# Down-projection weight loads of a mixture-of-experts loop issued by ScalarE instead of SyncE

## The reference, cut to what matters

```python
def expert_block(args):
    tok, e = args
    xb = t_pad[tok]
    hdn = jax.nn.silu(xb @ w_gate[e]) * (xb @ w_up[e])
    return hdn @ w_down[e]
```

## Time and profile before

| | us |
|---|---|
| median of 3 runs | 2498.84 (2497.75 to 2510.98) |
| the profiled execution's own time | 2495.0 |
| its span, first to last instruction | 2493.5 |
| TensorE matmul busy | 2087.8 (84%) |
| TensorE weight loads busy (beside the matmuls) | 1250.4 (50%) |
| VectorE busy | 1192.6 (48%) |
| ScalarE busy | 491.0 (20%) |
| GpSimd busy | 106.6 (4%) |
| DMA, mean over the span | 265 GB/s |

### The profile page before, as it was taken

One profiled execution on the slowest core, in us unless ns is written; L12 is line 12 of the kernel. 1 busy time (PEld: TensorE's weight loads), 2 busy tenths in 40 slices (PEclk: granted clock), 3 DMA queues, 4 the chain that ended last, 5 costly groups with the idle time before them and its releaser, 6 DMA issues. The chain is left out here.

```text
span 2493.5 us, 27613 instructions
## 1 busy us (share of the span) xinstructions
PE 2087.8 (84%) x9926; PEld 1250.4 (50%) x9926; DVE 1192.6 (48%) x1851; ACT 491.0 (20%) x513; POOL 106.6 (4%) x147
## 2 busy tenths in 40 slices
PE   0893898999999999989579966988888888888888
PEld 0211686777777777777368854333333333333332
DVE  0205667777777777777445454322222233222223
ACT  1103233333233333333234421000000000000000
POOL 0000000000000000000064000000000000000000
PEclk9997899999999999999789967999999999999999
DMA  3593565647465656566355543999999999999997
GB/s 121 168 305 101 171 183 159 207 139 223 136 209 153 197 157 193 157 194 186 139 175 198 186 169 140 421 422 422 422 422 422 422 422 422 422 422 422 422 422 322
DMA packets 300553, 660.45 MB, mean 265 GB/s; under 512 B 19984, under 2 KB 190480, under 8 KB 246112
## 3 DMA queue, kind: packets, MB, share of 16 engines
q1 hardware_dynamic: 293696, 635.51, 68.9%
q0 software_dynamic: 6672, 24.29, 2.8%
q10 hardware_dynamic: 144, 0.10, 0.0%
HBM read 653.33 MB, written 6.52 MB: 265 GB/s over the span
## 5 line engine op out<-in xcount | busy, mean ns | idle before, releaser
L1495 PE MATMUL bank<-wt,xe 128*64 128x512 f32 x2048 | 464.6, 595 | 111.9 <-DMA wt<-in_moe_w_up 108.5
L1301 PE MATMUL bank<-hTh,whi 128*128 128x512 f32 (+1 forms) x1296 | 455.6, 352 | 82.0 <-DVE wlo L832 59.8
L1302 PE MATMUL bank<-hTl,whi 128*128 128x512 f32 (+1 forms) x1296 | 446.3, 344 | 0.0
L1303 PE MATMUL bank<-hTh,wlo 128*128 128x512 f32 (+1 forms) x1296 | 445.9, 344 | 0.0
L1228 DVE TENSOR_TENSOR x<-x,bank 128x512 f32<-128x512 f32 x256 | 158.4, 681 | 544.6 <-PE bank L1482 544.6
L1495 PEld LDWEIGHTS bank<-wt,xe 128*64 128x64 f32 x2048 | 157.8, 136 | 412.8 <-issue 409.1
L1301 PEld LDWEIGHTS bank<-hTh,whi 128*128 128x128 f32 x1296 | 253.6, 196 | 130.3 <-issue 77.8
L1302 PEld LDWEIGHTS bank<-hTl,whi 128*128 128x128 f32 x1296 | 254.1, 196 | 26.5
L1303 PEld LDWEIGHTS bank<-hTh,wlo 128*128 128x128 f32 x1296 | 253.0, 195 | 27.8
L1520 PE MATMUL bank<-wt,hdn 128*64 128x512 f32 x1024 | 226.8, 595 | 1.4 <-DVE hdn L1240 1.4
L832 DVE TENSOR_TENSOR wlo<-raw,whi 128x2048 fp32r<-128x2048 f32 x81 | 185.2, 2287 | 82.3 <-ACT whi L636 80.4
(11 more groups left out here) (273 smaller groups left out, 1873.1 us busy)
## 6 DMA issues: line engine op xcount, KB each, us to landing
wt<-in_moe_w_gate SPq DMA_DIRECT2D x128, 1024.0 KB, 23.4
wt<-in_moe_w_up SPq DMA_DIRECT2D x128, 1024.0 KB, 25.5
wt<-in_moe_w_down SPq DMA_DIRECT2D x128, 1024.0 KB, 22.4
raw<-in_ada_w SPq DMA_DIRECT2D x96, 1024.0 KB, 5.0
raw<-in_ssm_w_in SPq DMA_DIRECT2D x81, 1024.0 KB, 5.8
raw<-in_ssm_w_out SPq DMA_DIRECT2D x32, 1024.0 KB, 4.8
bc<-cum_d POOLq DMA_DIRECT2D x32, 512.0 KB, 5.0
y_d<-ybuf POOLq DMA_DIRECT2D x32, 128.0 KB, 4.6
```

What stands on the lines that cost most here:

```text
L1301: pe.matmul(bank[:, 0:width], wh[:, k, :], hTh[:, k, 0:width], start=(k == 0), stop=False)
L1302: pe.matmul(bank[:, 0:width], wh[:, k, :], hTl[:, k, 0:width], start=False, stop=False)
L1303: last = pe.matmul(bank[:, 0:width], wl[:, k, :], hTh[:, k, 0:width], start=False, stop=(k == KC - 1))
L1495: last = pe.matmul(banks[0][SLOTS * h:SLOTS * h + SLOTS, :], xe[:, k, :], wt[2 * q + h][:, FF * i:FF * i + FF], start=(k == 0), stop=(k == ...
```

## The change

The function `down` and the waits of its loads move from SyncE's program to ScalarE's. SyncE keeps the gate and up loads. The waits (`s_xg` for block 0, `s_dn` for the rest), the buffers and the semaphores that the loads raise are the same. ScalarE now reads the block's expert number itself in every turn of the loop. Nothing changes on TensorE, VectorE and GpSimd.

```diff
@@ SyncE
-            def down(e, f):
-                sp.dma_start(wt[2 * NQ + f][:, :], w_down[e, :, f:f + 1, :].rearrange("o p f n -> (o p) (f n)")
-                             ).then_inc(s_wt[2 * NQ + f], 16)
...
             sp.wait_ge(s_xg, KC)
-            for f in range(FC):
-                down(slice(0, 1), f)
             for h in range(2):
...
                 for j in range(2 * NQ):
                     sp.wait_ge(s_gu[j % 2], b * NQ + (j // 2 + 1 - NQ))
                     up_gate(bass.ds(e, 1), j)
-                for f in range(FC):
-                    for h in range(2):
-                        sp.wait_ge(s_dn[h], b * FC + (f + 1 - FC))
-                    down(bass.ds(e, 1), f)
@@ ScalarE
+            def down(e, f):
+                act.dma_start(wt[2 * NQ + f][:, :], w_down[e, :, f:f + 1, :].rearrange("o p f n -> (o p) (f n)")
+                              ).then_inc(s_wt[2 * NQ + f], 16)
+
+            act.wait_ge(s_xg, KC)
+            for f in range(FC):
+                down(slice(0, 1), f)
             act.wait_ge(s_tab, 1)
...
             expert(0)
             with act.Fori(1, nblk) as b:
+                e = act.value_load(itab[0:1, bass.ds(b, 1)], min_val=0, max_val=NE - 1)
+                for f in range(FC):
+                    for h in range(2):
+                        act.wait_ge(s_dn[h], b * FC + (f + 1 - FC))
+                    down(bass.ds(e, 1), f)
                 expert(b)
```

## The result

| | us |
|---|---|
| kernel before, median of 20 runs | 2497.65 (2491.2 to 2510.98) |
| changed kernel, median of 20 runs | 2511.53 (2497.83 to 2522.74) |
| ratio | 1.0053, 95% interval 1.0038 to 1.0068 |
| the profiled execution's own time, before and after | 2495.0 and 2520.34 |
| span, before and after | 2493.5 and 2518.6 |

A forecast was written before the change was run, and what follows sets the result against it. The expert loop was taken as bound by its loads at 422 GB/s, with TensorE having 4.2 us to spare per block. Terms 0 + 0 + 0 + 8.8 + 0 on 2498.84 gave 2507.6 us, range 2497.0 to 2516.0.

The forecast's parts named there:

- The two issue terms: SyncE issuing four loads fewer and ScalarE four more per block: each worth 0 on the path.
- Down loads in another ring: End of the kernel: down loads pass waiting pairs, so the last pair lands 8.8 us later, at 2474.8 instead of 2466.0.
- the ends of 6.7 and 9.9: Bounds on the last pair's later landing: 6.7 us without any wait in that block, 9.9 as the latest possible.
- The fixed point of the working: End of the loads: total bytes are unchanged and engines never idle, so the last byte still passes at about 2473.7.
- The 27 to 74: Split of bytes between GpSimd's and SyncE's queues in an earlier row, set against the even split used for the sum.
- TensorE's clock: Last pair: a gathered 4.2 us wait might lower the clock, costing 0 to 3 us; taken as 0.
- the latest landing together with the slow clock: End of the kernel: 9.9 + 3 us, another way to the slower side; loss of rate or slow clock had 0.21.
- the slower rival: Slower by over 0.5%: rate lost with two rings, 2513.5 us, or latest landing with slow clock; chance 0.21.
- Nothing moves: Rival: loads served in issue order or pairs first; last up load lands at 2466.0, time 2498.8; chance 0.14.
- The engines lose rate with two rings: Rival in the loop: 418 GB/s against 422 costs 5.9 us, with the tail 14.7, so 2513.5; chance 0.21 including slow clock.
- A gain in rate: Rival in the loop: two rings raise the rate 3.5% to 437 GB/s, for a time of 2486; chance 0.05.
- The sum: Whole kernel: 0 + 0 + 0 + 8.8 + 0, giving 2507.6 us, counted as the same.

The follow-up runs named there:

- the short fill: Changed kernel plus 6 filling matmuls on TensorE ahead of the last block's last pair of loads: median 2508.29 us, ratio 1.0032, loop time 965.2 us.

## Why the prediction was right, and where it was not

*The two issue terms, 0 and 0: right.* SyncE's up issue fell from a median of 602 ns to 381, as its queue pushes back less, and that was worth nothing. ScalarE took its four issues without delay to anyone:

```profile
2465.84 5.49 ACTq L754 DMA_DIRECT2D wt<-in_moe_w_down  x4
2495.07 0.60 ACT L766 ACTIVATE gsb<-bank 128x512 f32<-128x512 f32 x1 [33.17 <-PE bank L1496]
```

From the end of the last issue at 2471.3 to the copy there are 23.7 us of room, and the copy waits for TensorE, not the reverse.

*Down loads in another ring, 8.8 us: right in mechanism, measured 9.2*, inside the ends of 6.7 and 9.9. The fixed point of the working held best: the last byte passes 936.1 us behind the loop's start, expected 935.9. That the two figures lie within 0.4 us is in part luck, as two details inside the working were off and cancelled. The first down issue of the last block came at 2465.84, 915.0 us into the loop, 2.1 earlier than the 917.1 that 2473.7 - 18.8 gives. The last pair's load landed 22.35 us after it instead of 19.9, as the block's waits were 0.80 + 6.28 and not 4.2. That load took 28.64 us from its issue, more than the 26 that the prediction gave as the most. Four down loads of a block, issued over 5.15 us, land as follows:

```profile
DMA to landing us min/median/max: 9.1/14.0/17.8
```

So the fourth landed 23 us behind the first issue. An even split with nothing left over from before gives 19.9 and the 2.2 us of landing, 22.1. The Trainium skill, page "DMA: Bandwidth & Descriptors", section "Queues, rings and completion order", has each DMA engine take turns between its rings by packet. By that rule the split is even, and this trace agrees to about 1 us, and by the bytes of each ring while both had work:

```profile
q10 hardware_dynamic: 344, 2.56, 51.1%
q1 hardware_dynamic: 341, 2.51, 50.2%
```

These are packets, MB and share from 2471 to 2483 us. The 27 to 74 of the earlier trace rows, between GpSimd's queue and SyncE's, did not hold for these two. The order of single packets is not visible here. The section "Issuing engines are not separate DMA queues" of that page of the Trainium skill has it that several issuing engines save only issue time. The unchanged 422 GB/s bears out that nothing is gained, but the sentence leaves out what decided here: loads in different rings land in another order.

*TensorE's clock, taken as 0 of 0 to 3: wrong, and the one step that failed.* The text said "I take 0, as 4.2 is nearer to 3.42". Both halves fail. The wait was not 4.2 us in each block: it gathers in every second one, and the last block has 0.80 + 6.28 us. In a group of four blocks near the end the waits of some 0.8, 6.3 and 3.7 us, with two slow pairs at 3 us extra each, make up the 16.8 us that TensorE has to spare. And 3.42 us was no bound: behind a wait of 3.70 us the clock fell here, and behind shorter ones too (last section). Nor did the row with 5.24 us of the earlier trace rows show a fall: the clock had stood at 0.50 well before it.

```profile
1460.00:1500.00 40.00, 22.77 (x96) 18.79 (x96) 20.54 (x61) 10.75 (x20) 0.00 (x0) 0.50 0.28 108
1500.00:1516.00 16.00, 3.79 (x16) 2.81 (x16) 13.26 (x41) 0.00 (x0) 0.00 (x0) 0.50 0.00 1
```

The size "up to 3 us" was right: 6.61 - 3.65 = 2.96, and the short fill took 2.6 of it back. I had named "the latest landing together with the slow clock" as a side branch of the slower rival. That is nearly what happened (9.2 + 3.0), and it belonged in the forecast.

*Nothing moves: refuted*, by down loads that land after 13.1 us and not 22.4, and by the last block's row.

*The engines lose rate with two rings: refuted.* From 1700 to 2400 us of the changed kernel:

```profile
DMA packets 40543, 295.30 MB, mean 422 GB/s; under 512 B 4498, under 2 KB 4498, under 8 KB 4498
...
q1 hardware_dynamic: 26901, 195.86, 67.2%
q10 hardware_dynamic: 13642, 99.44, 34.1%
```

The kernel before moves 295.35 MB in the same stretch. The 418 against 422 GB/s on which I had built that rival was another transfer shape and a rounded row. *A gain in rate* falls by the same lines.

*The sum.* 8.8 was forecast, the loop shows 12.1, and the medians 13.9 (12.7 when the change was run once more). 2507.6 was 3.9 us under the median measured, 2511.53. Whether the change counts as slower by over 0.5% stays on the edge: the ratio is 1.0053, and its interval holds 1.005.

## What to carry to other kernels

Where a loop is bound by its loads and their queue is always full, moving some of them to a second ring changes nothing in when the last byte passes, but it changes who lands last. Look at the end: whatever starts the longest chain of work behind its landing must not share the last bytes with loads that are wanted later. If two rings are used, give each an equal share of every step in the order of use, small slow transfers included; then it cost nothing here (loop 955.5 us against 955.7). And when waits change from many short ones to few long ones, price TensorE's clock at the place where the chain ends (3.0 us at the last pair here, about 0.1 where a later load had to be waited for anyway), and ask on which block it ends.

## What was not expected of the hardware

*The same idle time can come before a fall of the clock or not.* Every kernel here has the same idle time of 3.42 or 3.43 us ahead of the loop. In 11 of the 13 profiles the matmuls behind it ran at full clock, as in the earlier trace rows. In two, that of both rings in the order of use and that of the change with 31 blocks, the clock was at its lower level for a part of the first block: 15.65 us for 64 matmuls instead of 13.95. In the loop, every wait of 3.70 us or more was followed by a slow pair, and so were two of 3.06 and 3.07 us. With one down quarter in the other ring each block but the first two has a wait of 2.40 to 2.58 us, 30 in all, and the clock fell behind 17 of them and not behind the other 13. Of waits of up to 1.94 us ahead of a pair none was followed by a slow one. Yet a single wait of 1.95 us was, in the 31-block run of the changed kernel, which has another of 1.95 us without a fall:

```profile
1877.67 5.35 PE L1496 MATMUL bank<-wt,xe 128*64 128x512 f32 x16 [1.95 <-DMA wt<-in_moe_w_up]
```

So with idle times of 1.95 to 3.43 us it went either way in these runs, and a single row at 3.42 us, as I had used it, is no bound. The Trainium skill, page "TensorE: Matmul & The Clock Gate", part 1, reports that the number of slow matmuls at a kernel's start varies from run to run of one kernel. That fits the start of the loop here: behind 3.42 or 3.43 us of idle time the changed kernel had no slow matmul in both of its profiles, and with 31 blocks, whose code differs up to there in one small VectorE instruction, it had some.

*A small transfer can hold all DMA engines.* The gate vector's 0.5 MiB took 2.7 us from the loop, where 0.5 MiB of weights pass in 1.24 us. The engines' busy share stayed at 1.04 to 1.05 while the rate fell to 223 GB/s. Why these transfers are slow was not taken apart here.
